# Taking the expert outputs out of PSUM with VectorE, gate and modulation row in one instruction, in a mixture-of-experts block on one Trainium2 core

## What is computed

```python
xl = xl + mod_l[2] * yl
hl2 = rmsnorm(xl, norm2_w[i]) * (1 + mod_l[4]) + mod_l[3]
f = moe_ffn(hl2.reshape(-1, d), w_router, router_bias, w_e1[i], w_e3[i], w_e2[i])
xl = xl + mod_l[5] * f.reshape(xl.shape)
...
return rmsnorm(xl, final_norm_w)
```

## Time and profile before

| what | us |
|---|---|
| median of 3 runs | 2251.96 |
| the profiled execution itself | 2254.91 |
| its span, first to last instruction | 2253.3 |
| expert loop, one turn | 35.1 |
| TensorE busy, share of the span | 96% |
| mean granted TensorE clock | 0.983 of full speed |

### The profile page before, as it was taken

The page is one execution under the profiler, slowest core; times in us unless marked ns, Lnnn a source line. Parts: engine busy times, 40 slices in busy tenths (PEclk is TensorE's granted clock), DMA queues, the critical chain, the costliest instruction groups (busy, mean ns, idle before and its releaser), DMA issues.

```text
span 2253.3 us, 36303 instructions
## 1 busy us (share of the span) xinstructions
PE 2164.7 (96%) x12376; PEld 1767.6 (78%) x12376; DVE 1557.0 (69%) x1943; ACT 992.7 (44%) x1216; POOL 530.5 (24%) x672
## 2 busy tenths in 40 slices
PE   4889999999999999999999999999899999999996
PEld 2679878887887887788888888788688888888883
DVE  2478555666567656766666766743688989889897
ACT  3344323233333324322222222332268888888882
POOL 0046434553555354111111111100010010110101
PEclk8999999999999999999999999999899999999998
DMA  9975563222223223667677766834499999999998
GB/s 388 395 214 155 157 201 87 87 84 86 77 86 92 78 86 105 213 218 251 215 227 243 223 221 204 274 130 146 169 382 409 414 416 421 417 419 418 417 385 262
DMA packets 324751, 533.45 MB, mean 237 GB/s; under 512 B 12464, under 2 KB 247472, under 8 KB 294736
## 3 DMA queue, kind: packets, MB, share of 16 engines
q1 hardware_dynamic: 290976, 393.91, 49.0%
q0 software_dynamic: 33712, 138.71, 17.5%
HBM read 493.74 MB, written 36.73 MB: 235 GB/s over the span
## 4 chain that ended last, share of the span: by engine, by line
PE 81%; DVE 4%; issue 2%; DMA 2%; POOL 1%; ACT 0%; DVEq 0%; ACTq 0%; POOLq 0%
PE ps L715 13%; PE ps L717 12%; PE ps L716 12%; PE ps L1070 7%; PE ps L1068 7%; PE ps L1069 7%; PE ps L947 3%; PE ps L946 3%; PE ps L948 3%; PE ps L1005 2%; PE ps L1007 2%; PE ps L1006 2%; PE ps L1094 1%; DMA y_buf<-block_outputs,dest_i 1%; PE ps L825 1%
## 5 line engine op out<-in xcount | busy, mean ns | idle before, releaser
L1666 DVE TENSOR_TENSOR w_lo<-raw,w_hi 128x1024 fp32r<-128x1024 f32 x272 | 349.2, 1284 | 355.1 <-ACT w_hi L1229 353.5
L1229 ACT CAST w_hi<-raw 128x1024 fp32r<-128x1024 f32 x272 | 285.1, 1048 | 582.7 <-PE ps L717 277.8
L715 PE MATMUL ps<-hl_hi,w_hi 128*128 128x512 f32 x1280 | 505.8, 395 | 3.6 <-DVE hl_lo L1732 1.4
L717 PE MATMUL ps<-hl_hi,w_lo 128*128 128x512 f32 x1280 | 498.8, 390 | 0.0
L716 PE MATMUL ps<-hl_lo,w_hi 128*128 128x512 f32 x1280 | 498.5, 389 | 0.0
L2121 DVE TENSOR_TENSOR e_lo<-e_raw,e_hi 128x1024 fp32r<-128x1024 f32 x357 | 421.4, 1219 | 44.2 <-ACT e_hi L1510 36.9
L1510 ACT CAST e_hi<-e_raw 128x1024 fp32r<-128x1024 f32 x357 | 369.2, 1058 | 72.4 <-PE ps L1070 72.3
L715 PEld LDWEIGHTS ps<-hl_hi,w_hi 128*128 128x128 f32 x1280 | 240.3, 188 | 54.7 <-issue 3.4
L717 PEld LDWEIGHTS ps<-hl_hi,w_lo 128*128 128x128 f32 x1280 | 240.2, 188 | 50.7
L716 PEld LDWEIGHTS ps<-hl_lo,w_hi 128*128 128x128 f32 x1280 | 240.5, 188 | 47.9
L1068 PE MATMUL ps<-e_hi,xe_hi 128*128 128x512 f32 x512 | 201.2, 393 | 0.1
(11 more groups left out here) (388 smaller groups left out, 3593.8 us busy)
## 6 DMA issues: line engine op xcount, KB each, us to landing
e_raw<-in_w_e SPq DMA_DIRECT2D x192, 1024.0 KB, 9.8
raw<-in_w_in SPq DMA_DIRECT2D x208, 512.0 KB, 3.8
ada<-in_w_ada POOLq DMA_DIRECT2D x64, 1024.0 KB, 6.7
ada_ring<-in_w_ada SPq DMA_DIRECT2D x32, 1024.0 KB, 15.5
raw<-in_w_out SPq DMA_DIRECT2D x32, 512.0 KB, 3.7
block_outputs<-y_sb POOLq DMA_DIRECT2D x30, 512.0 KB
block_outputs<-osq POOLq DMA_DIRECT2D x1, 8192.0 KB, 27.6
raw<-in_w_branch_hgrn SPq DMA_DIRECT2D x16, 512.0 KB, 3.8
```

The source lines that it names most:

```text
L715: mm(dst, hi, rhs_hi[:, k, :], start=(k == 0), stop=False)
L717: last = mm(dst, lo, rhs_hi[:, k, :], start=False, stop=(k == KT - 1))
L1229: act_e.copy(w_hi[:, hslot, :], raw[:, slot, :]).then_inc(hi_done, 1)
L1666: tt(w_lo[:, hslot, :], raw[:, slot, :], w_hi[:, hslot, :].bitcast(F32), ALU.subtract).then_inc(split_done, 1)
```

## The change

The copies of block outputs (y_copy on ScalarE) are taken out. VectorE instead runs y_rows: four scalar_tensor_tensor that multiply a PSUM bank by the gate and by m5_row and write y_sb. In the loop they stand at the end of its turn; for block 14 after unit 20. Before the loop VectorE waits for m5_row and gate_tab. Block 15 is taken out in the same way into v_last, and its four operations stand before the joins. The modulations of y_buf in the tail are gone, x2 of tile 2 is added by TensorE's identity matmul, and only tile 3 gets it by a transfer, directly after its adding gather. VectorE's order in the tail is now join 0 and 1, then sum and finish of tile 0, of tile 1, sum 2, sum 3, finish 2 and 3.

```diff
...
@@ -1180,18 +1179,20 @@
             for i in range(NTOK):
                 banks = ((0, 1, 6, 7), (2, 3, 4, 5))[i % 2]
                 if i == 1:
-                    pe.wait_ge(v_gated, USED + 4)
-                if i < 2:
+                    pe.wait_ge(v_out, USED + 4)
+                if i == 2:
+                    pe.wait_ge(f_sum, 2)
+                if i < 3:
                     for n in range(4):
                         mm(bank(banks[n]), ident[:], x2[:, i, n * 512:(n + 1) * 512], start=True, stop=False)
                 for half in range(2):
-                    if i >= 2:
-                        pe.wait_ge(f_sum, 2 * (i - 2) + half + 1)
+                    if i == 3:
+                        pe.wait_ge(f_sum, 2 + half + 1)
                     for n in (2 * half, 2 * half + 1):
                         if i == 0:
                             pe.wait_ge(v_out, USED + n + 1)
                         last = mm(bank(banks[n]), slots_last[:, i, :], v_last[:, n * 512:(n + 1) * 512],
-                                  start=(i >= 2), stop=True)
+                                  start=(i == 3), stop=True)
                     last.then_inc(last_mm, 1)
 
 
...
@@ -1522,17 +1522,6 @@
                 act_e.wait_ge(act_T, b + 1)
                 act_e.copy(actT_hi[:].rearrange("p k t -> p (k t)"), bank(6)).then_inc(actT_hi_rdy, 1)
 
-            def gate_of(b):
-                return gate_tab[:, b:b + 1] if isinstance(b, int) else gate_tab[:, ds(b, 1)]
-
-            def y_copy(b, turn, units):
-
-                act_e.wait_ge(e_units, units)
-                act_e.wait_ge(y_out, turn * 32 + 16 * NTOK)
-                for part in range(4):
-                    activate(y_sb[:, part * 512:(part + 1) * 512], bank(2 + part), ACT.Copy, scale=gate_of(b)
-                             ).then_inc(y_ev, 1)
-
             AHEAD = EH - 1
             for q in range(AHEAD):
                 e_hi_unit(q, q, 16 * (q // 2 // EP + 1))
...
@@ -1579,15 +1567,9 @@
                 if u == AHEAD + 9:
                     act_e.wait_ge(e_units, G_LAST + EH + 8)
                     sig1(LAST)
-                if u == AHEAD + 17:
-                    y_copy(LAST - 1, LAST - 1, G_LAST + EH + 16)
             act_hi(LAST)
             for u in range(29, 32):
                 last_hi(u)
-            for n in range(4):
-                act_e.wait_ge(e_units, G_LAST + EH + 28 + 4 * (n // 2))
-                activate(v_last[:, n * 512:(n + 1) * 512], bank(2 + n), ACT.Copy, scale=gate_of(LAST)
-                         ).then_inc(v_gated, 1)
             n_extra = act_e.value_load(route_i[0:1, 7:8], min_val=0, max_val=NXTRA)
             with act_e.If(n_extra > 0):
                 with act_e.Fori(0, NXTRA) as b:
...
@@ -2244,6 +2225,19 @@
                 tt(actT_lo[:].rearrange("p k t -> p (k t)"), bank(6),
                    actT_hi[:].rearrange("p k t -> p (k t)").bitcast(F32), ALU.subtract).then_inc(actT_rdy, 1)
 
+            def gated(out, b, n):
+                gate = gate_tab[:, b:b + 1] if isinstance(b, int) else gate_tab[:, ds(b, 1)]
+                cols = slice(n * 512, (n + 1) * 512)
+                return stt(out=out[:, cols], in0=bank(2 + n), scalar=gate, in1=m5_row[:, cols], op0=ALU.mult,
+                           op1=ALU.mult)
+
+            def y_rows(b, turn, units):
+
+                dve.wait_ge(e_units, units)
+                dve.wait_ge(y_out, turn * 32 + 16 * NTOK)
+                for n in range(4):
+                    gated(y_sb, b, n).then_inc(y_ev, 1)
+
             AHEAD = EH - 1
             for q in range(1, AHEAD):
                 e_lo_unit(q, q)
@@ -2259,6 +2253,8 @@
                 if q in (10, 12, 14, 15):
                     x_lo(1, (10, 12, 14, 15).index(q))
             gate_up(0, EH + 16, True)
+            dve.wait_ge(rows_in, 7 * 16)
+            dve.wait_ge(table_rdy, 2)
             with dve.Fori(1, LAST) as e:
                 for q in range(24):
                     n = q + AHEAD
@@ -2271,6 +2267,7 @@
                         gate_up(e, e * 24 + (EH + 8))
                     if 18 <= q <= 21:
                         x_lo(e + 1, q - 18)
+                y_rows(e - 1, e - 1, e * 24 + (EH + 16))
 
             def last_lo(u):
                 load, half = last_raw(u)
@@ -2285,6 +2282,8 @@
                     act_lo(LAST - 1)
                 if u == AHEAD + 9:
                     silu(LAST)
+                if u == AHEAD + 15:
+                    y_rows(LAST - 1, LAST - 1, G_LAST + EH + 16)
             gate_up(LAST, G_LAST + EH + 24)
             own.wait()
             for i in range(NTOK):
@@ -2294,8 +2293,14 @@
             dve.nop().then_inc(slots_rdy, 1)
             for u in range(29, 32):
                 last_lo(u)
-            dve.wait_ge(rows_in, 7 * 16)
-
+
+            def last_out(half):
+                dve.wait_ge(e_units, G_LAST + EH + 28 + 4 * half)
+                for n in (2 * half, 2 * half + 1):
+                    gated(v_last, LAST, n).then_inc(v_out, 1)
+
+            last_out(0)
+            last_out(1)
             n_extra = dve.value_load(route_i[0:1, 7:8], min_val=0, max_val=NXTRA)
             with dve.If(n_extra > 0):
                 with dve.Fori(0, NXTRA) as b:
...
@@ -2331,39 +2337,20 @@
                     stt(out=o[:, cols], in0=o[:, cols], scalar=stat2[:, 3, i:i + 1], in1=fn_row[:, cols],
                         op0=ALU.mult, op1=ALU.mult).then_inc(o_rdy, 1)
 
-            def modulate_y(i):
-                tt(y_buf[i][:], y_buf[i][:], m5_row[:], ALU.mult).then_inc(y_mod, 1)
-
-            def last_out(half):
-                for n in (2 * half, 2 * half + 1):
-                    cols = slice(n * 512, (n + 1) * 512)
-                    dve.wait_ge(v_gated, USED + n + 1)
-                    tt(v_last[:, cols], v_last[:, cols], m5_row[:, cols], ALU.mult).then_inc(v_out, 1)
-
             def join(i):
                 dve.wait_ge(y_in[i], 32)
                 tt(y_buf[i][:], y_buf[i][:], y_pair[i][:], ALU.add).then_inc(y_joined, 1)
 
             join(0)
-            last_out(0)
             join(1)
-            last_out(1)
             dve.wait_ge(y_joined, USED + 1)
-            modulate_y(0)
+            whole(0)
+            finish(0)
             dve.wait_ge(y_joined, USED + 2)
-            modulate_y(1)
-            dve.wait_ge(y_mod, USED + 1)
-            whole(0)
+            whole(1)
+            finish(1)
             dve.wait_ge(y_in[2], 16)
-            modulate_y(2)
-            dve.wait_ge(y_in[3], 16)
-            modulate_y(3)
-            finish(0)
-            dve.wait_ge(y_mod, USED + 2)
-            whole(1)
-            dve.wait_ge(y_in[2], 32)
             whole(2)
-            finish(1)
             dve.wait_ge(y_in[3], 32)
             whole(3)
             finish(2)
@@ -2622,9 +2609,8 @@
             gather_y(1, 2, y_buf[2], ALU.add).then_inc(y_in[2], 16)
             pool.wait_ge(y3_in, Y3_IN + 16)
             gather_y(1, 3, y_buf[3], ALU.add).then_inc(y_in[3], 16)
-            for i in (2, 3):
-                pool.wait_ge(y_mod, USED + i + 1)
-                pool.dma_start(y_buf[i][:], x2[:, i, :], accum_op=ALU.add).then_inc(y_in[i], 16)
+            pool.wait_ge(y_in[3], 16)
+            pool.dma_start(y_buf[3][:], x2[:, 3, :], accum_op=ALU.add).then_inc(y_in[3], 16)
 
 
 
```

More of the change, by code:

```diff
@@ L455, in build @@
             [sem(f"y_in{i}") for i in range(NTOK)], sem("f_sum"), sem("o_rdy"), sem("o_out"))
-        v_gated, v_out, slots_rdy, last_mm, y_mod, y_joined, USED = (
-            c_sig_f, ff_taken, c_kgT_rdy, c_v_T, c_v_ev, c_kg_b, HEADS)
+        v_out, slots_rdy, last_mm, y_joined, USED = ff_taken, c_kgT_rdy, c_v_T, c_kg_b, HEADS
         y3_in, Y3_IN = rows_in, 7 * 16
@@ L1203, in _ @@
             act_e.sem_inc(gh_rdy, 1)
-            act_e.sem_inc(y_ev, 4)
             act_e.wait_ge(vecT_rdy, 1)
@@ L1565, in _ @@
                         x_hi(e + 1, q - 18)
-                y_copy(e - 1, e - 1, e * 24 + (EH + 16))
             def last_hi(u):
@@ L1602, in _ @@
                             act_hi(b + E)
-                    y_copy(b + E, b + LAST, b * 24 + (E * 24 + EH + 24))
             act_e.nop()
@@ L1623, in _ @@
             for s, n in ((ctx_state, 1), (hg_rdy, 1), (ph_rdy, 1), (m_rdy, 1), (row_rdy, 1), (ada2_free, 2),
-                         (w_ev, 4), (x2_rdy, 4), (m4_rdy, 1), (e_split, 2 * EP), (xe_rdy, 2), (actT_rdy, 2)):
+                         (w_ev, 4), (x2_rdy, 4), (m4_rdy, 1), (e_split, 2 * EP), (xe_rdy, 2), (actT_rdy, 2), (y_ev, 4)):
                 dve.sem_inc(s, n)
@@ L2310, in _ @@
                             act_lo(b + E)
+                    y_rows(b + E, b + LAST, b * 24 + (E * 24 + EH + 24))
             dve.nop()
```

## The result

The kernel became slower. In one comparison, the kernel before took 2252.57 us (median of 9 runs, 2251.78 to 2255.16) and the changed one 2257.64 us (9 runs, 2255.39 to 2262.18): a ratio of 1.0024, with an interval of 1.0015 to 1.0032. The forecast was 2246.1 us, faster. The two profiled executions have spans of 2253.3 and 2255.4 us.

The account below looks back on a forecast made before the run. The prediction took TensorE to bound the loop, with VectorE having the least room, and transfers and VectorE's work to set the tail. Loop 0 plus tail -5.9 took the median 2251.96 to 2246.1 us, range 2243.8 to 2250.5.

Parts of the forecast that it names:

- part 1: Expert loop: y rows move from ScalarE to VectorE, four operations of 0.67 us each, hidden in a gap; cost 0.
- the gap: VectorE idle for 2.71 us before the first e_lo of a turn, awaiting ScalarE's e_hi; claimed to hide the four new operations.
- VectorE becomes the loop's bound: End of each turn: new operations cost more than the gap, from 0.84 us each; 2266 us, chance 0.08, small version 0.03.
- the rival of full durations: Loop: VectorE operations take full durations, 37.0 us a turn against 35.1; 2273 us, chance 0.03.
- the tail gives less: Tail: joins behind the last rows and tile 3's transfers shrink the gain to 3.0 us; 2249 us, chance 0.22.
- the two new waits ahead of turn 1: Before the loop: VectorE waits for the modulation row and gate, with 9.5 us to spare; cost 0.
- Block 14's rows: VectorE, after unit 20: store and gathers 0.9 us earlier, bounds 0 and 1.2; TensorE's last unit at about 2211.7.
- The tail: After TensorE's last unit: VectorE ends at 2243.6 instead of 2249.45, worth -5.9 us, bounds -6.4 and -3.9.
- VectorE only 0.5 us behind it: Tail: x2 of tile 3 is the next late thing, landing at 2235.3, with VectorE 0.5 us behind.
- The waits of finish 0 and finish 1: Tail, VectorE: both finishes now wait for ScalarE's squares, 2.2 us each, returning part of the gain.

Follow-up runs that it names:

- the tail alone: The changed kernel with ScalarE copying the loop's y rows as before, gate only, modulation row left out for blocks 0 to 14; 2248.75 us, ratio 0.9978.
- the late window: The changed kernel with a 128x1 VectorE memset behind e_lo of q = 6 in each turn; 2250.22 us, one profiled run.
- the early window: The changed kernel with a 128x1 VectorE memset behind the second e_lo of each turn; 2248.77 us, ratio 0.9982.
- the three profiles with the gather ahead of the store: The changed kernel with POOL's token gather before the store, twice, then also with tile 1's join behind tile 0's sum; 2250.64, 2249.01, 2249.07 us.
- e2: The changed kernel with POOL issuing the token gather right after the token turn, ahead of the y rows' store; 2250.64 us, ratio 0.9988.

## Why the prediction was wrong, point by point

**The step that failed** is in part 1: "POOL's store comes about 0.7 us later in a turn and has 30 us", and with it "I book 0 for the 14 turns". It looked at one of POOL's instructions in the turn, the store, and not at the copy and the gather queued behind it, and it took their durations for fixed, whatever VectorE runs beside them. Before, the two stores fell into the gap (2093.19 and 2094.39, with VectorE idle until 2094.62), and copy and gather got through between the first e_lo behind it, in 0.77 and 1.14 us. The store did come 0.7 us later (3.17 us into TensorE's turn instead of 2.44) and cost nothing by itself. But with the gap filled the copy behind it starts in the second e_lo of the run instead of the first, and copy and gather are each held to the end of their run in 11 of 13 turns. Whether they got through before because VectorE had just been idle, or only because of where they started, no run separates. What the runs showed in place of 0: +7.4 us in the trace of after (13 x 0.57), because the token rows land 8.7 us later with 8.3 us to spare; all of it is given back by a window of 60 ns.

The rival "VectorE becomes the loop's bound" has the right stage and sign but not the mechanism: its point of decision was 0.84 us for each new operation, and they read 0.74, 0.66 from start to start, and VectorE's busy time in a turn stays under its length. That same row (2096.22, four until 2098.86) is against the rival of full durations. The rival "the tail gives less" came true in part (below).

**What was right in the loop.** The duration of the new operations (0.67 forecast), their place, e_lo on time (the first behind the gap starts 3.71 us into TensorE's turn, 3.87 before), the two new waits ahead of turn 1 at no cost (VectorE's first e_lo of turn 1 follows the operation before it without a gap, 0.60 us from start to start), and a TensorE busy for 35.1 of 35.1 us once POOL was out of the way.

**Block 14's rows.** Counted from TensorE's last unit, the first gather started 17.14 us ahead of it (2217.38 less 2200.24) instead of 16.41: 0.7 us earlier, where -0.9 for the gather and +0.2 for the unit, so 1.1 us together, had been forecast.

**The tail.** From the end of TensorE's last unit to VectorE's end it took 37.9 us before (2249.45 less 2211.54), 34.2 after, 33.6 in the tail alone and with the late window, 38.3 with the early one (the wait of 6.84 us above), and 31.6, 31.6 and 31.4 in the three profiles with the gather ahead of the store. The forecast was 31.9 (2243.6 less 2211.7). In the traces the sum was thus right where POOL isn't held up, and 2.3 us too good for the change as it was made; the medians, below, don't confirm that difference. In the trace of after the difference starts on POOL; the adding gather of tile 2 and the x2 transfer of tile 3 in after, then VectorE around them:

```profile
2219.36 3.53 POOL L2595 DMA_INDIRECT y_buf<-block_outputs,dest_i  x1 [9.85 <-DMA y_buf<-block_outputs,dest_i]
2223.20 1.87 POOL L2595 DMA_INDIRECT y_buf<-block_outputs,dest_i  x1 [0.30 <-issue]
2235.92 0.92 POOL L2613 DMA_DIRECT2D y_buf<-x  x1 [10.86 <-DMA y_buf<-block_outputs,dest_i]
```

```profile
2219.12 4.49 DVE L2342 TENSOR_TENSOR y_buf<-y_buf,y_pair 128x2048 f32<-128x2048 f32 x2
...
2227.99 0.15 DVE L2331 TENSOR_SCALAR stat<-stat 128x1 f32<-128x1 f32 x1 [2.11 <-ACTq L1595]
...
2243.28 2.35 DVE L2325 TENSOR_TENSOR x<-y_buf,ps 128x1024 f32<-128x1024 f32 x2 [2.71 <-DMA y_buf<-x]
```

The gather's issue meets the joins, which read two SBUF operands, is held until the second one starts (2221.33), and takes 3.53 us, where it took 1.63 before. All that hangs on it comes later by that, and sum 3 waits 2.71 us for x2. With the gather ahead of the store in the loop (e2), the same place in the tail falls better:

```profile
2210.78 1.61 POOL L2599 DMA_INDIRECT y_buf<-block_outputs,dest_i  x1 [10.10 <-DMA y_buf<-block_outputs,dest_i]
```

```profile
2233.20 2.35 DVE L2325 TENSOR_TENSOR x<-y_buf,ps 128x1024 f32<-128x1024 f32 x2 [0.16 <-DMA y_buf<-x]
```

It starts 0.80 us before the joins (2211.58) and sum 3 waits 0.16 us, which is the "VectorE only 0.5 us behind it" of the forecast. The waits of finish 0 and finish 1 for ScalarE's squares (2.11 us each) are those forecast at 2.2. The adding gather took 1.6 us in the three profiles with the gather ahead of the store in the loop and 3.3 to 3.7 in after, with either window and in the tail alone: what differs is where it starts, before the first join or within 0.01 us of its start in those three, and 0.05 to 0.44 us inside it in the others. Why it starts earlier in those three is open; no run was made for it, and each kernel has one profile.

By the medians the tail is worth less than by the profiles: the three kernels with the gather ahead of the store give -2.7, -3.6 and -3.5 us (the second, from its interval, -5.4 to -1.4) where the first one's profile reads -6.3 in the tail, against the 5.9 of the forecast. The two kernels whose adding gather is held, the early window and the tail alone, give -4.1 and -5.0 us by their ratios, so no less. The medians thus don't show that the hold in the tail costs anything; the 2.3 us are a reading of single profiles. Those are no fair sample: that of the kernel before lies above its median, that of the first kernel with the other order is the fastest of its ten, and a tail of the same code differed by 4 us (34.2 and 38.3). What of the forecast 5.9 us the tail really gives, 3 or 5, stays open; that it gives something is shown by all five kernels with a turn of 35.1 us that have it and were run ten times or more.

## What to carry to other kernels

Before you fill a gap on one engine, list what every other engine does in and behind that stretch, the small index copies and indirect gathers on GpSimd first, ask what they read and from where, and how late their results may come. Put an indirect gather where VectorE reads PSUM or waits anyway, not behind a long run of operations with two SBUF inputs; where the order can't be changed, try one tiny operation without an SBUF input in the run; here it opened the way. And an instruction that takes several times its usual time with unchanged operands is a sign to look at its neighbours' engine, not at its own.

## What the runs showed of the hardware

- A run of VectorE operations with two SBUF inputs holds up GpSimd instructions that read SBUF: a copy of 128x1 from 0.77 to 3.11 us, the issue of an indirect gather from 1.14 to 7.41 us. The issue of a plain transfer on the same engine stays at 0.55 us in the same stretch.
- Both get through at an operation of VectorE with one SBUF input or none: the copy ended 0.10 to 0.13 us behind the start of that operation, the gather's issue 0.92 to 0.96 us behind it. A memset of 128x1 that takes 0.06 us was enough in both places where it was tried.
- The Trainium skill, "SBUF — State Buffer", section "Who interferes with whom", says that a VectorE instruction with two SBUF inputs contends with a GpSimd instruction that reads SBUF, and one with at most one SBUF input does not, outside the modes that use both port pairs. The trace agrees on which operations hold and which let through (rows 2100.41 and 2104.35 above). It differs on the length: the page has the lock held for one instruction, and here the hold went on over three e_lo for the copy and six for the gather, the one in which it began counted. Of the tail's adding gather the page's length is true: it was held for one join.
- Not every run of such operations holds. In the kernel before, in turns 1 and 3 of after and behind the early window, POOL got through between two plain e_lo, and in the tail of after between two joins (the gather's issue ended 1.57 us behind the second's start). Turns 3 and 13 of after can't be told apart by their order: the copy starts 0.4 us into the second e_lo in both (1779.62 and 2100.41) and takes 0.83 us in one and 3.11 in the other. ScalarE's casts lie alike too: the e_hi of the next e_lo was ready 0.81 us before that second e_lo in both (1778.39 and 2099.18). What decides there stays open; no run was made for it.
